# A hybrid decoder step on Trainium2: the gate work at the beginning of the mixing stage, reordered

## The reference

```
lf  = log_sigmoid(f);  b = cumsum(lf) within a chunk
Dm  = b[t] - b[s] + i[s], causal
m_t = max(b + m_prev, max_s Dm);   w = exp(Dm - m_t)
num = (q k^T * w) v + exp(b + m_prev - m_t) * q C
ws  = exp(b_L - b + i - m_new);    sc = exp(b_L + m_prev - m_new)
C   = sc * C + (k * ws)^T v;       the same for n
```

## Time and profile before

| what | value |
|---|---|
| median of 3 runs | 2606.36 us (2605.89 to 2611.3) |
| profiled execution | 2602.27 us, span 2600.2 us |
| TensorE busy | 2477.8 us, 95% of the span |
| VectorE busy | 1314.2 us, 51% |
| ScalarE busy | 892.7 us, 34% |
| GpSimd busy | 409.4 us, 16% |
| granted TensorE clock, mean | 0.980 |

### The profile page before, as it was taken

One profiled execution on the slowest core, in us unless ns is written; L12 is line 12 of the kernel. 1 busy time (PEld: TensorE's weight loads), 2 busy tenths in 40 slices (PEclk: granted clock), 3 DMA queues, 4 the chain that ended last, 5 costly groups with the idle time before them and its releaser, 6 DMA issues.

```text
span 2600.2 us, 47024 instructions
## 1 busy us (share of the span) xinstructions
PE 2477.8 (95%) x17168; PEld 1957.5 (75%) x17168; DVE 1314.2 (51%) x2218; ACT 892.7 (34%) x2136; POOL 409.4 (16%) x242
## 2 busy tenths in 40 slices
PE   8999999999993999989999999998999999999998
PEld 6898898898883777757878888875666666666666
DVE  4656555323333466663236344335666666666653
ACT  4222121111111333323222111135666666666631
POOL 4224224323300000000004232200000000000031
PEclk9999999999996899989999999999999999999999
DMA  5233223224216399892232434359999999999972
GB/s 163 77 106 111 82 81 104 83 68 129 77 66 184 107 287 283 267 304 91 93 99 90 141 91 115 92 161 393 411 392 408 396 395 401 402 393 391 390 227 82
DMA packets 332228, 535.42 MB, mean 206 GB/s; under 512 B 30069, under 2 KB 241794, under 8 KB 328810
## 3 DMA queue, kind: packets, MB, share of 16 engines
q1 hardware_dynamic: 328962, 524.16, 57.7%
q10 hardware_dynamic: 3080, 8.82, 0.9%
HBM read 432.20 MB, written 100.56 MB: 205 GB/s over the span
## 4 chain that ended last, share of the span: by engine, by line
PE 87%; DVE 5%; DMA 2%; SPq 2%; ACT 1%; issue 1%; ACTq 1%; POOL 0%; DVEq 0%; POOLq 0%
PE at_ring L2846 8%; PE p_col L572 5%; PE p_col L574 5%; PE p_col L573 5%; PE p_gm L2275 4%; PE p_gm L2277 4%; PE p_gm L2276 4%; PE at_ssc L2878 4%; PE p_row L613 4%; PE at_ring L2867 4%; PE p_row L615 4%; PE p_row L614 4%; PE at_sc L2814 3%; PE at_ring L2836 3%; PE oa_out L1833 2%; PE oa_out L1835 2%
## 5 line engine op out<-in xcount | busy, mean ns | idle before, releaser
L2846 PE MATMUL at_ring<-ident,at_kp 128*128 128x128 f32 x2048 | 268.3, 277 | 14.8 <-DMA at_kp<-in_cache_k 9.7
L2846 PEld LDWEIGHTS at_ring<-ident,at_kp 128*128 128x128 f32 x2048 | 223.9, 141 | 59.1 <-issue 37.0
L572 PE MATMUL p_col<-h_hi,p_wqk 128*128 128x352 f32 x768 | 251.2, 327 | 1.1 <-DVEq L801 1.1
L574 PE MATMUL p_col<-h_hi,p_wqk 128*128 128x352 f32 x768 | 247.3, 322 | 0.0
L573 PE MATMUL p_col<-h_lo,p_wqk 128*128 128x352 f32 x768 | 247.0, 322 | 0.0
L2952 ACT ACTIVATE at_kT<-at_ring 128x512 f32<-128x512 f32 x384 | 218.3, 597 | 71.9 <-PE at_ring L2846 69.9
L613 PE MATMUL p_row<-p_wvz,h_hi 128*128 128x512 f32 x512 | 203.7, 398 | 3.4 <-ACT p_vst L696 3.4
L2275 PE MATMUL p_gm<-p_whl,h_hi 128*128 128x512 f32 x512 | 201.9, 394 | 0.9 <-DVE h_lo L2415 0.6
L615 PE MATMUL p_row<-p_wvz,h_lo 128*128 128x512 f32 x512 | 202.0, 394 | 0.0
L614 PE MATMUL p_row<-p_wvz,h_hi 128*128 128x512 f32 x512 | 201.2, 393 | 0.0
L2277 PE MATMUL p_gm<-p_whl,h_lo 128*128 128x512 f32 x512 | 199.4, 389 | 0.0
(11 more groups left out here) (407 smaller groups left out, 4876.8 us busy)
## 6 DMA issues: line engine op xcount, KB each, us to landing
at_kp<-in_cache_k SPq DMA_DIRECT2D x256, 512.0 KB, 7.6
at_vp<-in_cache_v SPq DMA_DIRECT2D x252, 512.0 KB, 7.5
s_qk<-p_res SPq DMA_DIRECT2D x32, 528.0 KB, 2.8
p_wst<-in_w_in_a SPq DMA_DIRECT2D x32, 512.0 KB, 3.8
p_wst<-in_w_in_a SPq DMA_DIRECT2D x64, 256.0 KB, 2.9
mx_qk<-s_qk SPq DMA_DIRECT2D x16, 1024.0 KB, 9.5
p_wst<-in_w_in_c SPq DMA_DIRECT2D x64, 256.0 KB, 4.6
s_v<-p_vst SPq DMA_DIRECT2D x64, 128.0 KB, 2.9
```

Of the source, the lines that this page charges most:

```text
L572: pe.matmul(out[:, r, 0:TN], wx[:, 0, k, :], h_hi[:, k, at], start=k == 0, stop=False)
L574: last = pe.matmul(out[:, r, 0:TN], wx[:, 1, k, :], h_hi[:, k, at], start=False, stop=k == KD - 1)
L2846: last = pe.transpose(bank("key", n, f)[:, h * PAGE:(h + 1) * PAGE], kp[n % 2][k][:, tile:tile + P], c.ident[:])
```

## The change

It moves the two conv stores ahead of the last head of p0. In mx it gives ScalarE a one-element Exp ahead of its first wait. The running maximum M is one scan over all 1024 prompt columns: the first operand, formerly zeros, is rows 1 set to zero, with the last b of the chunk before at the first column of each chunk but the first (`steps`), so that the sum carries from chunk to chunk. ml and mp are then copied and added for all chunks at once. em and the diagonals come later in VectorE's order. The 27 turns become three sets of nine (A, WS, EM) in PSUM tiles of the loop (`pt` is now a table of bcu and bnum[0], `pb` is bnum[1]), each with its own count. spread_m(0), the turn of A, the first third of the sample spreads, turn_k(0, 0) and scores(0, 0) now stand ahead of the rest. Of the loads, t_qk and t_v move behind qk(0, 1) and get a semaphore of their own, the tables kout, decay and gin move ahead of qk(0, 1), and t_state(0) moves behind v(0). Two semaphores more are cleared with the stage's pool.

```diff
@@ -540,16 +540,15 @@
             head(H - 1, H - 1, False, (0, True))
             with sp.Fori(H, HEADS - 1) as m:
                 head(m, m - H, True, (m - H + 1, True))
+            sp.wait_ge(tail_saved, 4 * H)
+            sp.dma_start(c.out["conv_p"][0, 0], tail_rows[0:NR, :]).then_inc(s_end, 16)
+            sp.dma_start(c.out["conv_s"].rearrange("a b r n -> (a b r) n"),
+                         tail_rows[NR:NR + DB * NR, :]).then_inc(s_end, 16)
             head(HEADS - 1, H - 1, True, None)
             for s in range(2):
                 sp.wait_ge(res_stored[s], 16 + 32 * HEADS)
                 sp.wait_ge(v_stored[s], 16 + 16 * HEADS * PER[s])
                 sp.wait_ge(g_stored[s], 16 + 16 * HEADS * PER[s])
-
-            sp.wait_ge(tail_saved, 4 * H)
-            sp.dma_start(c.out["conv_p"][0, 0], tail_rows[0:NR, :]).then_inc(s_end, 16)
-            sp.dma_start(c.out["conv_s"].rearrange("a b r n -> (a b r) n"),
-                         tail_rows[NR:NR + DB * NR, :]).then_inc(s_end, 16)
             sp.wait_ge(s_end, 32)
...
+        pt, pb = {A: bcu[:, 0], WS: bcu[:, 1], EM: bnum[0]}, bnum[1]
...
             load_qk(0, 0)
-            sp.dma_start(t_qk[:], c.s_qk[:, :, T:NT].rearrange("n p t -> p n t")).then_inc(s_tconst, 16)
             sp.dma_start(t_rep[:].rearrange("p a t -> p (a t)"), c.tab["spread_s"]).then_inc(s_tconst, 16)
             sp.dma_start(n_rows[:], g["state_mlstm_n"][0].rearrange("b h k -> (b h) k")).then_inc(s_tconst, 16)
...
             sp.dma_start(t_idle[:], c.tab["idle_rows"]).then_inc(s_tconst, 16)
-            for r in range(4):
-                sp.dma_start(t_v[32 * r:32 * r + 32, :, 0:DK], c.s_v[T:NT, :].rearrange("t (h n) -> t h n", h=HH)).then_inc(s_tconst, 16)
-            load_t(0)
-            load_qk(0, 1)
-            load_v(0)
             sp.dma_start(kout[:], c.tab["kout"]).then_inc(s_late, 16)
             sp.dma_start(decay[:].rearrange("p h t -> p (h t)"), c.tab["decay"]).then_inc(s_late, 16)
             sp.dma_start(gin[:].rearrange("p h t -> p (h t)"), c.tab["gin"]).then_inc(s_late, 16)
+            load_qk(0, 1)
+            sp.dma_start(t_qk[:], c.s_qk[:, :, T:NT].rearrange("n p t -> p n t")).then_inc(s_tv, 16)
+            for r in range(4):
+                sp.dma_start(t_v[32 * r:32 * r + 32, :, 0:DK], c.s_v[T:NT, :].rearrange("t (h n) -> t h n", h=HH)).then_inc(s_tv, 16)
+            load_v(0)
+            load_t(0)
             load_qk(1, 0)
             load_qk(1, 1)
             load_v(1)
             load_t(1)
-            sp.wait_ge(gr_dve, 1)
+            sp.wait_ge(gr_dve, 2)
             sp.dma_start(c.out["m_p"].rearrange("a b h -> h (a b)"), mp[:, NCH:NCH + 1]).then_inc(gr_out, 16)
             sp.dma_start(c.out["m_s"][0].rearrange("b h -> h b"), mnew[:], allow_slow_non_contiguous=True).then_inc(gr_out, 16)
             sp.wait_ge(gr_out, 32)
...
         def tensor(pe):
-            pe.wait_ge(gr_dve, 2)
-            for n in range(NB + 1):
-                for q, x in ((A, a), (EM, em), (WS, ws)):
-                    pe.transpose(pt[0:rows_of(n), (n * 3 + q) * H:(n * 3 + q + 1) * H],
-                                 x[:, n * P:n * P + rows_of(n)], c.ident[0:H, 0:H])
...
+            def turn_gates(q, x):
+                for n in range(NB + 1):
+                    last = pe.transpose(pt[q][0:rows_of(n), n * H:(n + 1) * H],
+                                        x[:, n * P:n * P + rows_of(n)], c.ident[0:H, 0:H])
+                last.then_inc(gr_pe, 1)
+
+            def spread_rows(q, x):
                 for h in range(H):
                     pe.matmul(bx[0][:, (q * H + h) * S:(q * H + h + 1) * S], select[:, h, :], x, start=True, stop=True)
...
             pe.wait_ge(ready, 1)
+            pe.wait_ge(s_const, 32)
+            pe.wait_ge(gr_dve, 1)
             spread_m(0)
+            turn_gates(A, a)
+            spread_rows(0, rows[:, 0, T:NT])
             turn_k(0, 0)
             scores(0, 0)
+            pe.wait_ge(gr_ws, 1)
+            turn_gates(WS, ws)
+            pe.wait_ge(gr_dve, 3)
+            pe.matmul(pb[:, 0:2 * NCH * H], ones[:], diag[:].rearrange("h q n k -> h (q n k)"), start=True, stop=True).then_inc(gr_pe, 1)
+            pe.wait_ge(gr_ws, 2)
+            spread_rows(1, rows[:, 1, T:NT])
+            spread_rows(2, ws_rows[:])
+            pe.wait_ge(gr_ws, 3)
+            turn_gates(EM, em)
+            spread_in(0)
             turn_k(0, 1)
-            spread_in(0)
+            pe.wait_ge(s_tconst, 16 * 8)
+            pe.wait_ge(gates_done, 1)
...
+            last.then_inc(t_spread, 1)
             turn_k(0, 2)
             turn_k(0, 3)
             scores(0, 1)
             pe.wait_ge(t_wt_ready, 1)
+            pe.wait_ge(s_tv, 16 * 5)
             t_turn(0)
...
         def scalar(act):
+            act.activation(sc[0:1, 0:1], c.ident[0:1, 0:1], ACT.Exp)
             act.wait_ge(logs_ready, 1)
             act.activation(b[:], b[:], ACT.Exp).then_inc(gr_act, 1)
             act.wait_ge(gr_act, 1)
             act.activation(b[:], b[:], ACT.Ln, bias=1.0).then_inc(gr_act, 1)
             act.wait_ge(logs_ready, 2)
-            act.activation(rows[:, 1, :], rows[:, 1, :], ACT.Exp)
-            act.activation(em[:], em[:], ACT.Exp)
             act.activation(ws[:], ws[:], ACT.Exp).then_inc(gr_ws, 1)
+            act.wait_ge(logs_ready, 3)
             act.activation(sc[:], sc[:], ACT.Exp).then_inc(gr_act, 1)
-            act.wait_ge(gates_done, 1)
+            act.activation(rows[:, 1, :], rows[:, 1, :], ACT.Exp).then_inc(gr_ws, 1)
...
-            act.wait_ge(t_masked, 1)
-            for h in range(H):
-                last = act.activation(t_wt[:, h, :], t_wt[:, h, :], ACT.Exp, bias=cols[0:S, NB, A, h:h + 1])
-            last.then_inc(t_wt_ready, 1)
+            act.wait_ge(cols_ready, 1)
+            weights(0)
+            act.wait_ge(logs_ready, 4)
+            act.activation(em[:], em[:], ACT.Exp).then_inc(gr_ws, 1)
             act.wait_ge(s_late, 48)
-            weights(0)
+            act.wait_ge(cols_ready, 2)
             for i in range(4):
+                if i == 2:
+                    act.wait_ge(t_masked, 1)
+                    for h in range(H):
+                        last = act.activation(t_wt[:, h, :], t_wt[:, h, :], ACT.Exp, bias=cols[0:S, NB, A, h:h + 1])
+                    last.then_inc(t_wt_ready, 1)
                 take_k(0, i)
...
-            ch.link(dve.memset(zeros[:], 0.0))
+            steps = by_chunk(rows[:, 1, :], True)
+            ch.link(dve.memset(rows[:, 1, 0:T], 0.0))
...
             ch.link(dve.tensor_tensor_scan(b[:], reset[:], f, 0.0, ALU.mult, ALU.add))
+            for prompt, n0, n1 in ((True, 0, NB), (False, NB, NCH)):
+                ch.link(dve.tensor_copy(bl[:, n0:n1].unsqueeze(2), by_chunk(b, prompt)[:, :, -1:]))
+            ch.link(dve.tensor_copy(steps[:, 1:, 0:1], bl[:, 0:NB - 1].unsqueeze(2)))
             ch.link(dve.tensor_tensor(a[:], gates[:, 0, :], b[:], ALU.subtract))
+            ch.link(dve.tensor_tensor_scan(M[:, 0:T], rows[:, 1, 0:T], a[:, 0:T], 0.0, ALU.add, ALU.max))
...
+            ch.link(dve.tensor_scalar(rows[:, 0, :], M[:], -1.0, None, ALU.mult))
+            dve.sem_inc(gr_dve, 1)
+            ch.link(dve.tensor_copy(ml[:, 0:NB].unsqueeze(2), by_chunk(M, True)[:, :, -1:]))
             ch.link(dve.tensor_copy(ml[:, NB:].unsqueeze(2), mext[:, :, DS:]))
-
             ch.link(dve.memset(mp[:, 0:1], 0.0))
-            for n in range(NB):
-                ch.link(dve.tensor_tensor_scan(M[:, n * P:(n + 1) * P], zeros[:], a[:, n * P:(n + 1) * P],
-                                               mp[:, n:n + 1], ALU.add, ALU.max))
-                ch.link(dve.tensor_copy(ml[:, n:n + 1], M[:, n * P + P - 1:n * P + P]))
-                after = n + 1 if n < NB - 1 else NCH
-                ch.link(dve.tensor_tensor(mp[:, after:after + 1], ml[:, n:n + 1], bl[:, n:n + 1], ALU.add))
+            ch.link(dve.tensor_tensor(mp[:, 1:NB], ml[:, 0:NB - 1], bl[:, 0:NB - 1], ALU.add))
+            ch.link(dve.tensor_tensor(mp[:, NCH:NCH + 1], ml[:, NB - 1:NB], bl[:, NB - 1:NB], ALU.add))
             ch.link(dve.tensor_tensor(mnew[:], ml[:, NB:], bl[:, NB:], ALU.add))
             dve.sem_inc(gr_dve, 1)
-            ch.link(dve.tensor_scalar(rows[:, 0, :], M[:], -1.0, None, ALU.mult))
-            ch.link(dve.tensor_tensor(em[:], rows[:, 0, :], b[:], ALU.subtract))
-            for prompt, n0, n1, w in ((True, 0, NB, P), (False, NB, NCH, DS)):
-                shape = [H, n1 - n0, w]
+            chunks = ((True, 0, NB, P), (False, NB, NCH, DS))
+            for prompt, n0, n1, w in chunks:
+                ch.link(dve.tensor_tensor(by_chunk(ws, prompt), by_chunk(a, prompt),
+                                          ml[:, n0:n1].unsqueeze(2).broadcast_to([H, n1 - n0, w]), ALU.subtract))
+            dve.sem_inc(logs_ready, 1)
+            for prompt, n0, n1, w in chunks:
```

(72 more changed lines are left out.)

17 lines of the change are left out of this document (6 added, 11 removed).

## The result

The kernel after takes 2588.55 us in the median of 6 runs (2586.94 to 2589.41); the kernel before, in the same comparison, 2606.12 us (6 runs, 2599.69 to 2611.3). The ratio is 0.9933, with a 95% interval of 0.9921 to 0.9945: 17.6 us less. Forecast were 2589.2 us and a gain of 17.2.

A forecast was written before the change was run, and what follows sets the result against it. TensorE was taken to limit the loop, a serial stretch the mixing stage's beginning. Terms -2.9 - 1.3 - 20.8 + 9.4 - 1.6 = -17.2 us put the profile at 2585.1, the median 4.1 higher at 2589.2; range 2583 to 2597.

The forecast's parts named there:

- (a): End of the stage before mixing: conv stores issued ahead of the last head let the stage end earlier, -2.9 us.
- (b): Start of the mixing stage: a dummy Exp puts ScalarE's first table load under the gates' transfer, -1.3 us.
- (c): End of the scan of b to scores(0,0): single scan and new order take 11.6 us against 32.4, -20.8 us.
- (d): scores(0,0) to t_num(0): work formerly ahead of the scores comes here, 24.6 us against 15.2, +9.4 us.
- (e): Spreads of rows 1 and 2 behind scores(0,0): a short stretch at 2.4 GHz shortens them, -1.6 us.
- the cover of the mask: Before scores(0,0): VectorE's mask takes 4.9 us while TensorE needs 5.8, so it is hidden with 0.9 us to spare.
- Transfers: Loads ahead of the loop: 7.6 MB land by 833.6 us, wanted at about 845, so 12 us of slack.
- Rival 1: Prologue of the mixing stage: full clock from the first scores on, gain 24.3 us, 2582 us; chance 0.10.
- Rival 2: Prologue: more waits between engines than counted, gain 12 us, 2594 us; chance 0.16.
- Rival 3: Prologue: t_state(0), last of the loads, lands late; gain 13 us at 150 GB/s, none at 120; chance 0.06.
- Rival 4: Loop: clock stays at 0.50; over one whole chunk it costs 30 us, 2619 us; chance 0.04.
- signs of being wrong: TensorE waiting for a DMA in the prologue, a wait over 1 us before scores(0,0), or longer loop or later stages.

The follow-up runs named there:

- e1: Kernel after with the two conv stores put back behind the last head's stores; 2592.41 us, ratio 0.9953.
- e4: Kernel before with only the single scan over 1024 columns, all else in the old order; 2601.61 us, ratio 0.998.
- e0: Kernel after, unchanged, run again as a control; 2585.23 us, ratio 0.9926.
- e2: Kernel after without the one-element Exp that loads ScalarE's table early; 2589.84 us, ratio 0.9944.
- e3: Kernel after with the eight scans of 128 columns put back in place of the single scan; 2593.04 us, ratio 0.9959.
- e5: Kernel after with 60 products of the identity ahead of spread_m(0) to warm TensorE; 2587.33 us, ratio 0.9933.
- e6: Kernel after with VectorE's subtraction making a done five times instead of once, delaying the prologue; 2593.38 us, ratio 0.9952.
- e9: Kernel after with the prologue's tail reordered, TensorE warmed by 60 identity products and the mask made earlier; 2584.99 us, ratio 0.9925.
- e10: The kernel of e2 profiled a second time, without further edit; 2589.97 us in one run.
- e7: Kernel after with the loads back in the order of the kernel before, new order of work kept; 2593.48 us, ratio 0.9947.

## Why the prediction was right, step by step

| step | forecast | measured |
|---|---|---|
| (a) conv stores | -2.9 | -2.8 |
| (b) first table | -1.3 | -1.36 |
| (c) end of the scan of b to scores(0, 0) | 11.6 us, -20.8 | 11.7 us, -20.7 |
| (d) and (e) scores(0, 0) to t_num(0) | 24.6 less 1.6, +7.8 | 22.3 us, +7.1 |
| t_num(0) | -17.2 | -17.7 |
| median | 2589.2 us | 2588.55 us |

The mechanism was right in each term but for the cover of the mask (below), and e1 to e4 bear out the sizes of (a), (b) and the scan. That the median came within 0.7 us is luck in part: the interval of the ratio allows a gain of 14 to 21 us, e0 gave 19.1, two errors in (d) and (e) cancelled, and the forecast profile (2585.1) plus 4.1 us hit the median although the profile itself took 2588.58, as long as the median.

(a) Confirmed by the positions and by e1.

(b) Confirmed by the timeline and by e2; only the load does not lie under the gates' transfer, as forecast, but ahead of it (796.10). The Trainium skill ("ScalarE: Activation LUTs", What ACT_TABLE_LOAD costs) counts a drain of about 1.38 us with each switch; by it removing one would have brought 2.7. This case doesn't show it: the activation follows the load by 0.02 us, and taking the load away moved the rest by 1.36.

(c) Confirmed, and its parts are within 0.2 us of the forecast each (scan 2.29 for 2.3, turn of A 0.78 for 0.92, spread_m 2.04 for 1.87). One thing in it failed: VectorE's mask was to be ready 0.9 us early. The timeline of the kernel after has turn_k(0, 0) and the mask

```profile
821.36 1.11 PE L1276 MATMUL mx_bk<-ident,mx_qk 128*128 128x128 f32 x4
821.69 0.69 DVE L1549 TENSOR_TENSOR mx_wt<-mx_prep,mx_mask 128x512 f32<-128x512 f32 x1 [0.25 <-DVE mx_sc L1540]
```

and the scores at 822.59: 0.12 us behind TensorE's own end (822.47) and 0.21 behind the mask's (822.38), about the hop that stands between rows 0 and spread_m(0) (816.66 to 816.85). So the mask came last and there was no cover. In e3, where it ends 0.95 us earlier against spread_m(0), the scores start 0.33 us earlier against it; that is about what it costs. VectorE needed 5.7 us for the 4.9 of the forecast, the difference being 0.85 us of gaps between its steps that the sum left out. e5 shows the mask as the limit at once when TensorE is faster. e3 and e4 size the scan within (c) at 3.6 to 4.1 us.

(d) and (e) The mechanism of both was right, and both sizes were off, in opposite directions. e2 does the same work at 1.2 GHz throughout: from scores(0, 0) to t_num(0) it takes 25.1 us (850.17 - 825.03), for the 24.6 of (d). The pieces that were longer are turn_k(0, 3), 1.12 for 0.76, scores(0, 1), 3.43 for 3.24, and the six small products, 1.26 for 1.06; the 16 spreads were shorter, 3.25 for 3.55. The rows of before for the first two lie in the stretch at 0.84 and had run partly at the higher clock. The kernel after takes 22.3 us: the clock gave 2.9 and not 1.6. Besides the spreads (1.71; 3.25 in e2) part of the scores (3.14; 3.75), the turn of WS (0.61; 0.97) and the ones product (0.33; 0.63) ran at 2.4 GHz. And I took the stretch itself as given, from one window of one execution: 4 of the 11 executions in the new order (e2, e6, e9, e10) go without it. It should have been carried as a chance.

**Transfers.** No wait of TensorE for a DMA in the prologue, as forecast. My account of the loads named only t_state(0) as the one to watch, though; e7 shows that the place of kout, decay and gin was worth 4.4 us, because the work that needs gin came forward with the rest. The forecast was right as the diff moves them; it didn't say that this move carries part of the gain, and it counted bytes but not the time that SyncE's issues take.

**What makes the gain.** Of the 14.9 us behind the landing, the first table load is 1.4 (e2) and the single scan 3.6 to 4.1 (e4, e3). The remaining 9.5 to 10 are put down to the order of the work by difference, with 2.9 us of the stretch at 2.4 GHz in them, and on condition of the loads' new places (e7); no run has the new order alone, and none takes its parts apart. The conv stores add 2.8 ahead of the landing.

**The rivals.** Rival 1 (full clock throughout) is refuted by the windows after and by e5: even when raised beforehand, the clock was at 0.50 again ahead of the scores. The Trainium skill ("TensorE: Matmul & The Clock Gate", What's actually happening) has activity release the throttle. The trace, with TensorE busy 9.03 of 10 us at 0.55, doesn't bear it out for this work, most of it products of four rows. Rival 2 (more waits) didn't show: ahead of the scores TensorE waits 0.12 us by the chain, and behind them (d) was 0.5 us longer than forecast, most of it in operations. Rival 3 (t_state(0) late) didn't show; its mechanism exists for another load (e7). Rival 4 (half clock in the loop) didn't show: 1.00 from 852 us on. Of the signs of being wrong, one needs a word: the later stages were 4.0 us longer in the profile after (1741.6 us from t_num(0) on for 1737.6), but 0.8 shorter in e0, the same program.

## What to carry to other kernels

In a serial beginning of a stage, write the chain out step by step, move everything ahead of the first dense products that they don't need behind them, and price what comes back on the other side: here 20.7 us won on one side of scores(0, 0), 7.1 given back on the other. Each load whose consumer is moved forward has to move too, the small tables as well as the large tensors (4.4 us for three tables issued last). Read such a change at the first place behind it, and leave the worth to medians: two profiles of one kernel (after and e0) differed by 4.8 us between t_num(0) and the end, 1.8 of it with one stretch of clock that no edit had touched.
